# Two hybrid blocks in float32: two more weight chunks by seven block products, the pool output product by input halves with the convolution begun inside it, and the gate columns turned later

## What is computed

```python
u = rms_norm(h, norm_in_g)
proj = u @ w_in                                    # 1024 x 4096
pool_x, pool_z, m_x, m_z = split(proj)             # 1024 features each
y_pool = pool_mixer(pool_x) * silu(pool_z)         # window means, a 256x256 product per group
y_m = mlstm_branch(m_x, ...) * silu(m_z)
h = h + concat([y_pool, y_m]) @ w_out              # 2048 x 1024

def mlstm_branch(u, ...):
    c = silu(centred_depthwise_conv(u, conv_w, conv_b))   # 5 taps along the sequence
    q, k, v = headwise(c, w_q), headwise(c, w_k), headwise(u, w_v)
    gates = concat([q, k, v]) @ w_gates + b_gates  # needs c and m_x of all 1024 features
    ...                                            # bidirectional mLSTM, 4 heads, chunks of 128
```

## Time and profile before

| | us |
|---|---|
| median of 3 runs | 1176.48 (1175.88 to 1176.59) |
| the profiled execution | 1176.67 |
| its span | 1174.8 |
| PE busy in the span | 1148.3 (98%) |
| DVE, POOL, ACT busy | 724.0, 496.6, 382.1 |
| PE's share of the chain that ended last | 89% (DVE 7%) |

### The profile page before, as it was taken

How to read it: one execution, slowest core, us unless ns; L and a number is a source line. 1 busy time by engine, 2 the same in 40 slices (tenths; PEclk the granted TensorE clock), 3 DMA queues, 4 the chain that set the end, 5 groups by cost and what they waited for, 6 DMA issues and landing times.

```text
span 1174.8 us, 17393 instructions
## 1 busy us (share of the span) xinstructions
PE 1148.3 (98%) x6539; PEld 936.2 (80%) x6539; DVE 724.0 (62%) x1309; ACT 382.1 (33%) x750; POOL 496.6 (42%) x469
## 2 busy tenths in 40 slices
PE   8999999999999959999999999999999999999997
PEld 5888888888888837788878888888988887777786
DVE  5975347654435980247777882894799433556668
ACT  6522322221000122354765531232121134554322
POOL 4565642223324320444666667213323323455534
PEclk9999999999999979999999999999999999999999
DMA  7324242214534121300112342223131130133113
GB/s 240 117 63 144 90 132 84 81 36 132 184 108 143 36 72 63 109 19 24 41 45 57 133 180 65 79 73 121 37 90 36 37 99 2 37 114 131 38 36 143
DMA packets 82004, 101.97 MB, mean 87 GB/s; under 512 B 14209, under 2 KB 59481, under 8 KB 80898
## 3 DMA queue, kind: packets, MB, share of 16 engines
q1 hardware_dynamic: 74198, 97.12, 24.9%
q10 hardware_dynamic: 7724, 3.74, 1.1%
HBM read 79.30 MB, written 23.12 MB: 87 GB/s over the span
## 4 chain that ended last, share of the span: by engine, by line
PE 89%; DVE 7%; DMA 1%; issue 1%; POOL 1%; ACT 1%; ACTq 0%; DVEq 0%; SPq 0%; POOLq 0%
PE bank L1058 20%; PE bank L1060 20%; PE bank L1059 20%; DVE cva L1942 4%; PE bank L1374 3%; PE bank L1399 3%; PE wide L1060 2%; PE wide L1058 2%; PE wide L1059 2%; PE wide L1390 2%; PE wide L1592 2%; PE bank L1338 1%; PE bank L1327 1%; DVE cva L1938 1%; PE bank L1315 1%
## 5 line engine op out<-in xcount | busy, mean ns | idle before, releaser
L792 POOL CAST whi<-wraw 128x2048 fp32r<-128x2048 f32 x26 | 51.8, 1994 | 350.5 <-PE bank L1060 294.2
L1058 PE MATMUL bank<-u_hi,wlo 128*128 128x512 f32 x356 | 139.6, 392 | 3.3 <-ACT um L2687 3.3
L1059 PE MATMUL bank<-u_lo,whi 128*128 128x512 f32 x356 | 139.2, 391 | 0.0
L1060 PE MATMUL bank<-u_hi,whi 128*128 128x512 f32 x356 | 139.1, 391 | 0.0
L794 POOL TENSOR_TENSOR wlo<-wraw,whi 128x2048 fp32r<-128x2048 f32 x27 | 129.0, 4777 | 2.6 <-ACT whi L2887 0.5
L1058 PE MATMUL bank<-x_hi,wlo 128*128 128x512 f32 x312 | 123.5, 396 | 0.0
L1060 PE MATMUL bank<-x_hi,whi 128*128 128x512 f32 x312 | 121.6, 390 | 0.0
L1059 PE MATMUL bank<-x_lo,whi 128*128 128x512 f32 x312 | 121.5, 389 | 0.0
L1058 PEld LDWEIGHTS bank<-u_hi,wlo 128*128 128x128 f32 x356 | 67.2, 189 | 18.4 <-issue 4.5
L1060 PEld LDWEIGHTS bank<-u_hi,whi 128*128 128x128 f32 x356 | 67.3, 189 | 14.0
L1059 PEld LDWEIGHTS bank<-u_lo,whi 128*128 128x128 f32 x356 | 67.2, 189 | 14.0
(11 more groups left out here) (431 smaller groups left out, 2741.6 us busy)
## 6 DMA issues: line engine op xcount, KB each, us to landing
wraw<-in_w_in SPq DMA_DIRECT2D x21, 1024.0 KB, 5.4
wraw<-in_w_out SPq DMA_DIRECT2D x12, 1024.0 KB, 5.1
wraw<-in_w_in SPq DMA_DIRECT2D x12, 512.0 KB, 4.9
xr<-in_x SPq DMA_DIRECT2D x8, 512.0 KB, 7.2
hst<-in_x SPq DMA_DIRECT2D x4, 1024.0 KB, 5.2
hpool<-hst SPq DMA_DIRECT2D x4, 1024.0 KB, 4.1
h<-hpool SPq DMA_DIRECT2D x4, 1024.0 KB, 7.2
resid<-h SPq DMA_DIRECT2D x8, 512.0 KB, 2.6
```

What stands on the lines that cost most here:

```text
L792: g_.tensor_copy(whi[w % 2][:, :, :], wraw[:, :, :]).then_inc(s["w_hi"], 1)
L1058: pe.matmul(ps, al, bh, start=(k == 0), stop=False)
L1059: pe.matmul(ps, ah, bl, start=False, stop=False)
L1060: return pe.matmul(ps, ah, bh, start=False, stop=(k == nk - 1))
```

## The change

It has five parts.

1. **Seven instead of five chunks by block products.** Chunks 10 (m_x of head 2) and 13 (m_z of head 1) move up into `SEVEN`. Their results go to DRAM (`umraw`, `smz`). The slots of the weight blocks turn by two places, so that the first two blocks of the first chunk lie in the first `whi` and blocks 2 to 5 in the second.
2. **The half sums of T3 and T4** move from POOL to DVE.
3. **Pool's output product by input halves**: the order of its chunks is 0, 1, 2, 3. `hst` then goes to DRAM and back between all four (the partial sums of each column half are stored to `hpool` and loaded again), in two parts each.
4. **The convolution** is done in place in `cc` and begins inside the output product: one step behind each of the last 4 additions of the third chunk, two behind each of the 8 of the fourth (20 of 40 steps); `um` of heads 0 and 1 is loaded after the second chunk, that of head 2 after the fourth.
5. **The gate columns** are turned after the first head's `headwise` and `scores`, and the gate chain starts after half a group, not after one.

The diff, cut to its core:

```diff
-    plan = [("w_in", c, "f") for c in (0, 12, 8, 9, 6, 5, 4, 1, 2, 3, 7)]
-    plan += [("w_out_pool", c, "o") for c in (0, 2, 1, 3)]
-    plan += [("w_in", c, "f") for c in (10, 11, 13, 14, 15)]
+    plan = [("w_in", c, "f") for c in (0, 12, 8, 9, 10, 13, 6, 5, 4, 1, 2, 3, 7)]
+    plan += [("w_out_pool", c, "o") for c in range(4)]
+    plan += [("w_in", c, "f") for c in (11, 14, 15)]
...
-SEVEN = range(2, 7)
+SEVEN = range(2, 9)
...
+        def place(b):
+
+            return (b + 2) % 8
...
         def slot_free(b):
 
-            return ("t_gemm", 4 if b < 4 else 8) if b < 8 else ("t_prod", b - 7)
+            return ("t_gemm", 4 + 4 * (place(b) // 4)) if b < 8 else ("t_prod", b - 7)
...
-            def store_h(half, q):
-                sp_.wait_ge(s["v_hp"], 16 * half + 8 + 4 * q + 4)
...
+            def load_h(q, part):
+                if q:
+                    sp_.wait_ge(s[f"o_h{part}"], 16 * q)
+                src = x_v if q < 2 else hpool_d
+                sp_.dma_start(hst[:, rows_h(part), :], src[:, rows_h(part), cols_h(q % 2)]).then_inc(s[f"l_xh{part}"], 16)
+
+            def store_h(q, part):
+                sp_.wait_ge(s["v_hp"], 8 * q + 4 * part + 4)
+                sp_.dma_start(hpool_d[:, rows_h(part), cols_h(q % 2)], hst[:, rows_h(part), :]).then_inc(s[f"o_h{part}"], 16)
...
+            for part in range(2):
+                store_h(0, part)
+                load_h(1, part)
...
+            wt(W_OP + 3)
...
+            for part in range(2):
+                store_h(1, part)
+                load_h(2, part)
+            for i in range(2):
+                load_um(i)
+            wt(W_OP + 4)
+            for part in range(2):
+                store_h(2, part)
+                load_h(3, part)
             wt(W_OP + 5)
...
+            for part in range(2):
+                store_h(3, part)
+            load_um(2)
+            wt(W_OP + 6)
...
-            def first_half(i, k):
-                ks = slice(4 * k, 4 * k + 4)
-                g_.tensor_tensor(Tf[:, i, :, :], u_hi[:, ks, 0:HALF].bitcast(F32), u_lo[:, ks, 0:HALF].bitcast(F32),
-                                 ALU.add).then_inc(s["g_T"], 1)
-
-            g_.wait_ge(s["v_ulo"], 8)
-            first_half(T3, 0)
             g_.wait_ge(s["v_xn"], NT)
             split(1)
-            first_half(T4, 1)
...
+            begun = group(W_MZ + 2, 3, u_hi, u_lo, "a_mz", mz_count(11), ks=range(4))
+            pe.wait_ge(s["a_gsum"], 2)
...
             for b in range(2):
                 scores(0, b)
+            pe.wait_ge(s["a_r"], 6)
+            pe.wait_ge(s["v_r"], 4)
+            ps = fill("v_cols", 1)
...
-            second_half(T1, 0)
-            ve.wait_ge(s["g_T"], 1)
+            half_of(T1, 0, 1)
+            half_of(T3, 0, 0)
             combine(T1, full(T1), full(T3), ALU.subtract)
...
+                    ve.wait_ge(s[f"l_xh{t // 4}"], 16 * (q + 1))
                     ps = filled(ve, "t_gemm", first[W_OP + q] + t + 1, "v_hp", n + 1)
                     ve.tensor_tensor(hst[:, t, :], ps[:, :], hst[:, t, :], ALU.add).then_inc(s["v_hp"], 1)
-
-            ve.wait_ge(s["o_h0"], 32)
-            ve.wait_ge(s["o_h1"], 32)
...
+                    if n >= 20:
+                        conv_steps(1 if q == 2 else 2)
+            conv_steps(TAPS * KT - stepped[0])
```

More of the change, by code:

```diff
@@ L856, in _ @@
                 g_.wait_ge(s["g_blk"], 4 * c + 4)
-            for w in range(W_POOL[1], W_MX + 3):
+            for w in range(W_POOL[1], W_MX + 4):
                 split(w)
@@ L936, in units @@
                         heads_blocks(h + 1)
-            for w in range(W_MX + 4, W_OM + 1):
+            for w in range(W_MZ + 3, W_OM + 1):
                 split(w)
@@ L1252, in _ @@
                           ps=ring_x("v_hp", n) if q == 0 and i >= 4 else None)
-            for h in (2, 3):
-                for i in range(4):
-                    group(W_MX + h, i, u_hi, u_lo, "a_um", 4 * (h - 2) + i + 1)
             for i in range(4):
-                group(W_MZ + 1, i, u_hi, u_lo, "a_mz", 4 + i + 1)
+                group(W_MX + 3, i, u_hi, u_lo, "a_um", i + 1)
+            for n in range(8, 11):
+                group(W_MZ + 2, n % 4, u_hi, u_lo, "a_mz", mz_count(n))
             pe.wait_ge(s["v_ga"], 6)
@@ L1287, in _ @@
-            for i in range(4):
-                group(W_MZ + 3, i, u_hi, u_lo, "a_mz", 12 + i + 1)
-            pe.wait_ge(s["a_r"], 6)
-            pe.wait_ge(s["v_r"], 4)
-            ps = ring_x("v_cols", 1)
-            for n in range(4):
-                pe.transpose(ps[:, n * ROWS:(n + 1) * ROWS], r4[:, n, :], cst[0:ROWS, C_ID:C_ID + ROWS])
-            pe.matmul(ps[:, 4 * ROWS:5 * ROWS], ones[0:ROWS, :], rn[:, :], start=True, stop=True
-                      ).then_inc(s["t_rows"], 1)
+            begun = group(W_MZ + 2, 3, u_hi, u_lo, "a_mz", mz_count(11), ks=range(4))
@@ new lines, in _ @@
+            pe.wait_ge(s["a_gsum"], 2)
+            ps = ring_x("v_gs", 4)
+            for t in range(NT):
+                mm = pe.matmul(ps[:, t * 16:t * 16 + 16], gsum[:, t * P:(t + 1) * P],
+                               cst[:, C_SUM:C_SUM + 16], start=True, stop=True)
+            mm.then_inc(s["t_gate"], 1)
+            group(W_MZ + 2, 3, u_hi, u_lo, "a_mz", mz_count(11), ks=range(4, KT), ps=begun)
+            pe.wait_ge(s["v_gs"], 4)
+            ps = ring_x("v_rif", 1)
+            for kind in range(2):
+                mm = pe.transpose(ps[0:ROWS, kind * P:(kind + 1) * P],
+                                  gs[:, kind, :, :, :].rearrange("p d h c -> p (d h c)"), idn)
@@ L1298, in _ @@
+            mm.then_inc(s["t_rows"], 1)
+            for n in range(12, 16):
+                group(W_MZ + 3, n % 4, u_hi, u_lo, "a_mz", mz_count(n))
             turns, free = [0], [1, 5, 2, 6, 3, 7]
@@ L1408, in _ @@
                 scores(0, b)
+            pe.wait_ge(s["a_r"], 6)
+            pe.wait_ge(s["v_r"], 4)
+            ps = fill("v_cols", 1)
+            for n in range(4):
+                pe.transpose(ps[:, n * ROWS:(n + 1) * ROWS], r4[:, n, :], cst[0:ROWS, C_ID:C_ID + ROWS])
+            pe.matmul(ps[:, 4 * ROWS:5 * ROWS], ones[0:ROWS, :], rn[:, :], start=True, stop=True
+                      ).then_inc(s["t_rows"], 1)
             del free[1:]
@@ L2842, in _ @@
                 evac_scores(0, b)
+            ac.wait_ge(s["v_cols"], 1)
+            weight(0)
             for h in range(NH):
```

206 lines of the change are left out of this document (87 added, 119 removed).

## The result

The changed kernel takes 1183.2 us (median of 4 runs, 1180.37 to 1184.16), the kernel before beside it 1176.53 (4 runs, 1175.88 to 1177.79): ratio 1.0054, 95% interval 1.0035 to 1.0073. It is slower by 6.7 us where 6.5 us less were predicted. Its profiled execution took 1184.16 us, with a span of 1182.4.

A forecast was written before the change was run, and what follows sets the result against it. PE, busy 98% of the span, was taken as the bound, so only less PE work or fewer PE waits help: 1176.67 - 5.4 - 2.3 + 1.0 - 4.9 + 4.9 = 1170.0 us, range 1161 to 1176.5.

The forecast's parts named there:

- Then: store, 292.1; the next load and store, 299.6; ... the load for the fourth chunk, 343.3: Output product: SP's queue of hst transfers followed in order, putting the fourth chunk's load at 343.3, 5.7 us late.
- 5.0 for the first of two, 2.5 for each more: SP's queue: landing price in us of 1 MB transfers in a row, read from two transfers.
- With every transfer of the chain 1 us slower it is some 22, and PE is held for banks as well: Gate product: upper end for PE's wait, some 22 us, where 15.4 was taken.
- Rival D: Output product: hst round trips delay everything behind; gain used up if fourth chunk's load lands at 350.0; 1179 to 1184, chance 0.06.
- PE is not held yet (1.6 us spare): Output product, fourth chunk: PE, four banks ahead, needs DVE's late first addition only by 345.6, so does not wait.
- 2.3 us less: Block phase: PE's wait for a scaled tile of x goes once POOL's half sum no longer locks DVE.
- 1.0 us more: Block phase: DVE's two extra sums and rotated slots make low blocks late; between 0 and 3 us, 1.0 taken.
- 24 fewer matmuls: Block products: two more chunks with 84 instead of 96 matmuls each, 5.4 us less on PE.
- no wait for `um`: After the output product: PE's wait for an evacuation to `um` and the low clock behind it go, 4.9 us less.
- the convolution tiles hit by two splits: Convolution's last 20 steps: two POOL weight splits fall into them, each costing DVE 5.7 us.
- the columns: Later gate columns: PE's 0.7 us wait goes but a new chain stands there; 0.7 less to 2 more, 0 taken.
- the gate product's wait: Gate product: PE asks at 394.6, convolution done at 410.1, so PE waits 15.4 us, 4.9 more than the 10.5 before.

The follow-up runs named there:

- e1: Changed kernel with the twelve small gate-weight loads issued from ACT's queue instead of SP's; 1176.35 us, ratio to before 0.9991.
- e2: Changed kernel without the hst stores behind the first and second chunk, later chunks loading x again (result incomplete); 1171.46 us, ratio to before 0.9953.
- e3: Changed kernel with all 40 convolution steps behind the last addition of the output product; 1189.37 us, ratio to before 1.0107.
- e5: Changed kernel with SP issuing the two stores of the first m_z tiles ahead of the next block chunk's load; 1179.13 us, ratio to before 1.0021.
- e7: Changed kernel with POOL's split of the last m_z chunk held back until all convolution steps are done; 1177.83 us, ratio to before 1.0001.
- e8: Changed kernel with POOL's split of the first of the last two m_z chunks ahead of its wait for hst stores; 1184.61 us, ratio to before 1.0061.
- f3: Changed kernel with the output product's old column order (0, 2, 1, 3), 16 convolution steps inside it, head 2's um loaded earlier; 1169.6 us, ratio to before 0.9940.
- e6: Kernel before with only the half sums of T3 and T4 moved from POOL to DVE; 1178.19 us, ratio to before 1.0012.
- f4: f3 with the edits of e1, e5 and e7 and the later gate product of e4; 1160.98 us, ratio to before 0.9861.
- e4: Changed kernel with the gate product and what hangs on it one group of 24 matmuls later in PE's order; 1178.76 us, ratio to before 1.0017.

## Why the prediction was wrong

**What decides.** In all kernels with the changed kernel's order behind the gate product, the span from its start to the end is one number, whatever PE waited for ahead of it:

| kernel | gate product starts | wait there | span | span less start |
|---|---|---|---|---|
| changed | 460.35 | 10.5 | 1182.4 | 722.1 |
| e1 | 453.89 | 12.1 | 1175.0 | 721.1 |
| e2 | 448.44 | 9.2 | 1169.8 | 721.4 |
| e3 | 466.42 | 16.3 | 1187.7 | 721.3 |
| e5 | 456.98 | 9.4 | 1177.7 | 720.7 |
| e7 | 455.10 | 2.7 | 1176.1 | 721.0 |
| e8 | 462.26 | 15.8 | 1182.9 | 720.6 |
| f3 | 445.48 | 4.5 | 1167.0 | 721.5 |

The last column spans 1.4 us, and the clock behind the wait makes that difference: the first half of the gate product takes 4.9 us in e5 and e8 and 6.2 in the changed kernel, and without it the column agrees within 0.2 us. The prediction had this structure right and its part behind the gate product too (721.1). It had the start of the gate product wrong by 13.5 us: 3.3 ahead of the output product and 10.2 in the chain of `hst`.

**The step that failed: "Then: store, 292.1; the next load and store, 299.6; ... the load for the fourth chunk, 343.3".** Issue times of the trace less 40.07, against the prediction's:

| step | predicted | found | late |
|---|---|---|---|
| first store landed | 292.1 | 293.2 | 1.1 |
| load and store | 299.6 | 302.0 | 2.4 |
| gate weights issued | 308.3 | 312.1 | 3.8 |
| `wraw` and a store | 315.8 | 322.5 | 6.7 |
| a load and a store | 323.3 | 331.2 | 7.9 |
| load, two `um`, `wraw` and a store | 338.3 | 347.5 | 9.2 |
| fourth chunk's first addition | 343.3 | 353.95 | 10.7 |

From there on the chain held: the gate product starts at 460.35 - 40.07 = 420.28 against 410.1, 10.2 late. No step went wrong alone; each of the seven was 1.1 to 2.9 us too cheap. The first is a store by itself, 5.2 us where 4.1 stood. The third is mostly the issue of the gate weights, 9.6 us where 8.3 stood. The other five used the price "5.0 for the first of two, 2.5 for each more", which came from two loads, for loads and stores mixed. The dearest step, 10.4 for 7.5, is a store behind `wraw` and the twelve small loads, which landed in 9.7 us; in e1 the same store, with a load of `hst` and `wraw` just ahead of it, took 10.4 (343.73 to 354.12). What each transfer ahead adds is not separated.

The prediction had this case as its other end ("With every transfer of the chain 1 us slower it is some 22, and PE is held for banks as well"), but its range ends at 1176.5. Rival D had it right: the gain is used up at 350.0, and beyond it the kernel is slower one for one. The load came at 353.95, which makes 4.0 us, and 7.2 with the 3.3 ahead of it; the profiled execution is 7.5 us slower than before. Only D's condition did not come: the five transfers in a row took 16.3 us and not 24, and the delay was spread over all steps. D's chance of 0.06 rested on "the landings of 4.1 to 7.1 us were seen with one or two under way, and leave room"; that was a reason for a wide term, not for a small chance.

**"PE is not held yet (1.6 us spare)"** was wrong for the same reason: PE waits 1.2 us at 394.86. It waits longer, 5.67 us, for the third chunk, which the prediction did not look at: its partial sums came back 14 us after DVE was ready. These 7.1 us cost nothing by themselves, since PE then stands 10.5 us at the gate product all the same (e8 shows this for the wait of 3.0); what cost was DVE's chain.

**"2.3 us less", "1.0 us more".** The wait went, but its gain was returned in the second block chunk: 2.0 us in e6 where nothing else was changed, 2.8 in the changed kernel. The prediction looked at POOL's low blocks there, and no wait for one came. The chain that decides ran through ACT's first evacuation, which waits for a store of m_z, which SP's queue holds behind a load that waits for POOL (e5 moved it, and the wait went). The prediction also put nothing for the clock behind such a wait: 1.7 us here, as in e6. So the stretch up to the output product took 40.07 us more than before and not 36.8, and this is the second step that failed, with 3.3 us.

**Right:** 24 fewer matmuls (6515 against 6539 in the traces), no wait for `um`, the convolution tiles hit by two splits at 5.7 us each, DVE's 3.12 us for an addition and two steps (2.98 on average), and the columns at 0.8 where 0.7 stood. PE's busy time was to fall by 5 us and rose from 1148.3 to 1149.2, since matmuls at the lower clock count as longer work; in f4, at the highest granted clock of all (0.996), it is 6.4 below before.

That the gate product's wait was found at 10.5 and not at 15.4 is no success of the sum: two errors nearly cancel. The convolution ended 13.5 us later than predicted, and PE came 18.4 later (449.8 against 394.6 + 36.8 = 431.4): 3.3 ahead of the output product, 7.1 of waits for `hst`, 3.0 for the split, and some 5 for the lower clock behind them and small gaps. For the 5.4 us of saved matmuls to become a profit, the convolution's chain has to be out of the way, as f3 and f4 have it.

## What to carry to other kernels

Find the one event that the rest hangs on (here the start of the gate product) and predict its time along the chain that ends last in it; a wait removed upstream of it on another engine is worth nothing, and an error in one term of that chain, such as a store that must land before a load is issued, goes into the time in full. Price a row of transfers from a row that mixes the same kinds in the same queue, or give the term a range as wide as the difference. When another engine's task slows the engine on the path, as POOL's splits do with DVE's steps, let that task wait until the path is through: one added wait on POOL gained 5.4 us, as much as 24 fewer matmuls.

## What the runs showed of the hardware that was not expected

- A 1 MB store from SBUF landed in 4.1 to 5.2 us when no load had been issued on its queue in the 4.9 us ahead of it (all four stores of before and of e2, the first of the changed kernel), in 8.4 to 8.6 when a 1 MB load had been issued 0.4 us ahead (three stores of the changed kernel), and in 12.6 behind four of them, issued within 3.7 us.
- Issuing one such store took SP 3.20 us (375.04) and in e1 4.46 us, with four transfers of 1 MB outstanding, where others took 0.37 to 0.51.
- POOL's eight small products for `Amat` took 2.90 us in the changed kernel and 9.31 in f4, where DVE was in its convolution steps. It delays the split behind them by 6.4 us, and PE waits 5.7 for that split.
- The same program's front part differs between executions: the wait in the second block chunk was 2.7 to 3.1 us in seven profiles (changed kernel, e1, e2, e3, e7, e8, f3) and 0.75 in e4, whose code is the same up to there.
